# Up projections of two feed-forward blocks as seven block products instead of eight, over two halves of the tokens

## What is computed

```
def half_ffn(x, g, w_up, w_down):          # x: tokens x 1024, w_up: 1024 x 5632, w_down: 2816 x 1024
    a, b = jnp.split(rmsnorm(x, g) @ w_up, 2, axis=-1)
    return x + 0.5 * ((jax.nn.silu(a) * b) @ w_down)
```

## Time and profile before

| | us |
|---|---|
| median of three runs | 2714.2 (2714.13 to 2714.91) |
| the profiled execution, whole | 2714.25 |
| its span in the profile | 2712.2 |
| mean granted TensorE clock of that execution | 0.982 of full speed |
| TensorE busy | 2630.6 |
| VectorE, ScalarE, GpSimd busy | 1008.2, 726.6, 718.8 |

### The profile page before, as it was taken

How to read it: one execution, slowest core, us unless ns; L and a number is a source line. 1 busy time by engine, 2 the same in 40 slices (tenths; PEclk the granted TensorE clock), 3 DMA queues, 4 the chain that set the end, 5 groups by cost and what they waited for, 6 DMA issues and landing times. The chain is left out here.

```text
span 2712.2 us, 37487 instructions
## 1 busy us (share of the span) xinstructions
PE 2630.6 (97%) x15304; PEld 2563.0 (94%) x15304; DVE 1008.2 (37%) x2105; ACT 726.6 (27%) x1276; POOL 718.8 (27%) x400
## 2 busy tenths in 40 slices
PE   7999999999999999999998998998999999999998
PEld 6999999999998899999987778998999999999997
DVE  5022222221117237998635642324022222222116
ACT  5111111111113332212547753223111111111112
POOL 5222222222222211212223103325222222222221
PEclk8999999999998999999998998998999999999999
DMA  4111111111103221213333404512111111111102
GB/s 133 47 47 41 38 47 47 33 46 47 44 19 103 73 67 58 65 49 100 94 85 73 76 1 134 169 32 63 47 47 47 32 47 47 41 37 47 47 16 78
DMA packets 208890, 160.42 MB, mean 59 GB/s; under 512 B 34844, under 2 KB 192600, under 8 KB 208608
## 3 DMA queue, kind: packets, MB, share of 16 engines
q1 hardware_dynamic: 208736, 158.16, 20.1%
HBM read 130.94 MB, written 25.99 MB: 58 GB/s over the span
## 5 line engine op out<-in xcount | busy, mean ns | idle before, releaser
L372 PE MATMUL f1ps_up<-xn_lo,f1w_hi 128*128 128x384 f32 x1056 | 353.9, 335 | 8.5 <-POOL xn_lo L327 8.5
L372 PE MATMUL f2ps_up<-xn_lo,f2w_hi 128*128 128x384 f32 x1056 | 354.3, 335 | 7.1 <-POOL xn_lo L327 7.1
L373 PE MATMUL f2ps_up<-xn_hi,f2w_lo 128*128 128x384 f32 x1056 | 353.7, 335 | 0.0
L374 PE MATMUL f2ps_up<-xn_hi,f2w_hi 128*128 128x384 f32 x1056 | 353.7, 335 | 0.0
L373 PE MATMUL f1ps_up<-xn_hi,f1w_lo 128*128 128x384 f32 x1056 | 353.5, 335 | 0.0
L374 PE MATMUL f1ps_up<-xn_hi,f1w_hi 128*128 128x384 f32 x1056 | 353.5, 335 | 0.0
L372 PE MATMUL d_ps<-xn_lo,d_w_hi 128*128 128x384 f32 x864 | 298.6, 346 | 6.5 <-POOL xn_lo L327 4.9
L373 PE MATMUL d_ps<-xn_hi,d_w_lo 128*128 128x384 f32 x864 | 293.6, 340 | 0.0
L374 PE MATMUL d_ps<-xn_hi,d_w_hi 128*128 128x384 f32 x864 | 293.5, 340 | 0.0
L530 DVE TENSOR_TENSOR f2hid<-f2gate,f2ps_up 128x384 f32<-128x384 f32 x66 | 36.6, 555 | 503.2 <-ACT f2gate L499 503.2
L530 DVE TENSOR_TENSOR f1hid<-f1gate,f1ps_up 128x384 f32<-128x384 f32 x66 | 36.6, 555 | 503.1 <-ACT f1gate L499 503.1
(11 more groups left out here) (357 smaller groups left out, 5178.8 us busy)
## 6 DMA issues: line engine op xcount, KB each, us to landing
f1raw<-in_w_ffn_up SPq DMA_DIRECT2D x44, 512.0 KB
f2raw<-in_w_ffn_up SPq DMA_DIRECT2D x44, 512.0 KB
d_raw<-in_w_in SPq DMA_DIRECT2D x35, 512.0 KB, 5.1
p_dram<-stage SPq DMA_DIRECT2D x24, 576.0 KB, 3.2
f1raw<-in_w_ffn_down SPq DMA_DIRECT2D x11, 1024.0 KB
f2raw<-in_w_ffn_down SPq DMA_DIRECT2D x11, 1024.0 KB
b_sg<-p_dram SPq DMA_DIRECT2D x16, 576.0 KB, 4.9
x_dram<-xT SPq DMA_DIRECT2D x1, 4608.0 KB, 15.1
```

The source lines that it names most:

```text
L372: nc.tensor.matmul(out, w_hi, x_lo, start=first, stop=False)
L373: nc.tensor.matmul(out, w_lo, x_hi, start=False, stop=False)
L374: return nc.tensor.matmul(out, w_hi, x_hi, start=False, stop=final)
```

## The change

Both `ffn` calls are replaced. The token axis is cut into two halves of 576 (`HT`), each of two quarters of 288 (`QT`). The weights are loaded, and split, once for each half. A tile of an up projection is 1024 rows by 256 columns of `w_up`, seen as a 2 by 2 matrix of blocks (512 by 128); the normalised tokens of a half are a 2 by 2 matrix of blocks too (512 rows by 288 tokens). Their product takes seven block products (Strassen's scheme in the form with shared sums) where eight would do it directly. Four of the seven weight operands are differences of blocks (`terms`), four of the seven token operands are sums or differences (`combine`), and the four result blocks are sums of the seven products (`add`). One block product is 4 k-blocks by 3 matmuls of 288 columns, 12 matmuls; a down step is 12 matmuls of 288 columns as well (2 quarters, 2 hidden blocks, 3). The order of steps, for each half:

```diff
+    RING, RAWS, TS = 9, 3, 4
+    ORDER = [tile for g in range(NG) for tile in (("a", g), ("b", g), ("d", g - 1)) if tile[1] >= 0] + [("d", NG - 1)]
...
+    FREED = {LAST[j - RING]: j for j in range(RING, len(LAST))}
...
+    EDGE = STEP[0, "d", NG - 2]
```

On VectorE, which runs for every step s: `evict`, then `ahead(FREED[s])`, then `rest(s)`:

```diff
+                def terms(tile, which):
...
+                        if q:
+                            dve.wait_ge(t_ok, q)
+                        a, b = [(part(n, 0, 1), part(n, 0, 0)), (part(n, 1, 1), ts[:, (q - 1) % TS]),
+                                (part(n, 1, 1), part(n, 0, 1)), (part(n, 1, 0), ts[:, (q - 2) % TS])][i]
+                        v.tensor_tensor(ts[:, q % TS], a, b, ALU.subtract).then_inc(t_ok, 1)
...
+                        terms(tile, {0: (0, 1), 1: (2,), 4: (3,)}.get(x, ()))
...
+                    for dst, src in {1: ((1, 0),), 2: ((0, 0),), 3: ((2, 0),), 4: ((3, 2), (0, 0)), 5: ((0, 0),),
+                                     6: ((2, 2),)}[m]:
+                        v.tensor_tensor(ev[:, b + dst], ev[:, b + src], bank(s), ALU.add).then_inc(ad_ok, 1)
...
+                    v.tensor_tensor(product(x), ev[:, AT[x]], product(x), ALU.mult).then_inc(hm_ok, 1)
...
+                    dve.wait_ge(hh_ok, 4 * group(h, g) + x + 1)
+                    v.tensor_tensor(hidden(h_lo, h, g, x), product(x), hidden(h_hi, h, g, x).bitcast(F32), ALU.subtract)\
+                        .then_inc(hl_ok, 1)
...
+                    if kind == "d":
+                        dve.wait_ge(mm_ok, s + 1)
...
+                        v.scalar_tensor_tensor(x, ps[:, b:b + 2, 0:QT], 0.5, x, ALU.mult, ALU.add).then_inc(dn_ev, 1)
+                        return
+                    if m:
+                        add(G, s, kind, m)
+                    if kind == "b" and m in (1, 4, 5, 6):
+                        multiply(G, {1: 0, 4: 1, 5: 2, 6: 3}[m])
+                    if kind == "b" and m == 4:
+                        hidden_lo(h, g, 0)
+                    if kind == "b" and m == 6:
+                        hidden_lo(h, g, 1)
```

On the other engines:

```diff
+                def split_lo(j):
+                    pool.wait_ge(hi_ok, j + 1)
+                    nc.gpsimd.tensor_tensor(slot(w_lo, j), source(j), slot(w_hi, j).bitcast(F32), ALU.subtract)\
+                        .then_inc(lo_ok, 1)
+                    pool.wait_ge(lo_ok, j + 1)
...
+                def down(s, h, g, m):
...
+                    if 8 * G + m >= 2:
+                        pe.wait_ge(dn_ev, 8 * G + m - 1)
```

More of the change, by code:

```diff
@@ L374, in product3, with ffn @@
     return nc.tensor.matmul(out, w_hi, x_hi, start=False, stop=final)
-def ffn(nc, ctx, M, K, w_up, w_down, gain, xT, xn_hi, xn_lo, tag, summed):
+def ffn(nc, ctx, M, K, w_up, w_down, gain, xT, tag, summed):
     sem = lambda n: ctx.enter_context(nc.semaphore(tag + n))
[L387 to L391, removed]
-    with ExitStack() as mem, M.scope():
[L393 to L413, removed]
@@ L454, in run, with bank @@
[L454 to L471, removed]
+        def bank(s):
+            return ps[:, UPS.index(s) % 4, 0:QT]
@@ new lines, in added, with group, part, hidden @@
+        def added(G, kind, n):
+            return 14 * G + (7 if kind == "b" else 0) + n
+        def group(h, g):
+            return NG * h + g
+        def part(n, row, col):
+            r = raw[:, n % RAWS].rearrange("p (k n) -> p k n", k=KT)
+            return r[:, 4 * row:4 * row + 4, col * P:(col + 1) * P]
+        def hidden(t, h, g, x):
+            f, i = ((0, 0), (1, 1), (1, 0), (0, 1))[x]
+            return t[:, group(h, g) % 2, f, i * QT:(i + 1) * QT]
+        def product(x):
+            return ev[:, 4 + AT[x]]
@@ new lines, in _ @@
+                norm.root(act)
+                norm.rows(act)
+                for k in range(4):
+                    if k < 2:
+                        split_hi(k)
+                    for which in "ABS":
+                        norm.high(act, 0, k, which)
+                for j in range(2, RING):
+                    split_hi(j)
+                for s, step in enumerate(STEPS):
+                    evict(s, *step)
+                    if s in FREED:
+                        split_hi(FREED[s])
+                    rest(s)
@@ new lines, in _ @@
+                for k in range(4):
+                    if k < 2:
+                        split_lo(k)
+                    x_low(0, k, "A")
+                    x_low(0, k, "B")
+                for j in range(2, RING):
+                    split_lo(j)
+                for s, step in enumerate(STEPS):
+                    if s in FREED:
+                        split_lo(FREED[s])
+                    if EDGE <= s < EDGE + 16:
+                        k, r = divmod(s - EDGE, 4)
+                        if r == 1:
+                            x_low(1, k, "A")
+                            x_low(1, k, "B")
+                        if r == 3:
+                            x_low(1, k, "S")
@@ new lines, in _ @@
+                norm.inverse(dve)
+                norm.diagonals(dve)
+                for k in range(4):
+                    norm.apply(dve, 0, k)
+                    norm.combine(dve, 0, k, range(4))
+                    if k == 1:
+                        ahead(0)
+                    if k:
+                        norm.low(v, dve, 0, k - 1, "S")
+                norm.low(v, dve, 0, 3, "S")
+                for j in range(1, RING):
+                    ahead(j)
+                for s, step in enumerate(STEPS):
+                    evict(s, *step)
+                    if s in FREED:
+                        ahead(FREED[s])
+                    rest(s)
@@ L585, in project @@
+                norm.sums(pe)
+                norm.spread(pe)
+                for s, (h, kind, g, m) in enumerate(STEPS):
+                    if kind == "d":
+                        down(s, h, g, m)
+                    else:
+                        up(s, h, kind, g, m)
 def project(nc, ctx, M, K, io, out, xT, x_dram, xn_hi, xn_lo, kvT, DM, mix, aq_at, kvT_at, mix_at, scratch, g_dram, E):
```

477 lines of the change are left out of this document (329 added, 148 removed).

## The result

The kernel after takes 2902.4 us (median of 4 runs, 2901.1 to 2903.7), the kernel before 2714.4: a ratio of 1.069 (95% interval 1.067 to 1.071), slower by 188 us, where 2840 was forecast. The profiled execution spans 2900.6 us.

A forecast was written before the change was run, and what follows sets the result against it. TensorE's feed-forward matmuls were taken to bound the kernel. From 2714.25 us, -119.5 for fewer columns, +172 for stalls before d2, +36 for starts, +36 for middles and +1 for end evictions gave 2840; range 2640 to 2935.

The forecast's parts named there:

- Slower: Whole kernel: the chance given to the change making it slower, 0.71, against same 0.04 and faster 0.25.
- The lock of VectorE and GpSimd: Steady groups: VectorE operations with two SBUF operands and GpSimd's SBUF-reading ones exclude each other, delaying d2 by 4.3 us.
- VectorE keeps up: Rival, b tile: lock waits fit the slack, stall 0.1 us, up to 1.3; 2636 to 2690 us, chance 0.22.
- half the waits: Rival, b tile: stalls of only 2 to 3 us a pair; 2700 to 2780 us, chance 0.12.
- the hand schedule: b tile: both queues laid out one after the other, giving 5.4 us of lock waits for ten VectorE operations.
- the likeliest case: Whole kernel: VectorE late by the lock, 2790 to 2890 us, chance 0.50.
- the clock falls as well: Rival, after stalls before d2: half clock for 5 us costs 2.3 each, 92 in all; 2890 to 2935 us, chance 0.14.
- TensorE's columns: Feed-forward blocks: 5808 matmuls of 288 columns at 0.1315 us replace 4752 at 0.1733, saving 119.5 us (108 to 137).
- the left end of the line: Matmul time: 256 columns at mean 0.1175 us, joined by a line to 384 columns to give 0.1315 at 288.
- The stalls: d2 after a b tile: TensorE waits 4.3 us for VectorE's eviction of d0, 40 times, +172 us (4 to 196).
- The edges: Starts and middles: VectorE's list with lock waits delays TensorE, +18 us a block (10 to 24) and +18 (8 to 22).
- Hidden: Weight loads: loading twice, 69 MB a block at 81 GB/s, stays covered and costs TensorE nothing.

The follow-up runs named there:

- e1: Kernel after with GpSimd's subtraction for the weights' low parts replaced by a memset that reads nothing (output lacks them): 2674.6 us, 0.985 of the kernel before.
- e9: e1 with three more memsets per weight slot, keeping GpSimd about as busy as in the kernel after but reading nothing: 2676.2 us, 0.986 of the kernel before.
- e10: Kernel after with each GpSimd subtraction for a weight slot made as two instructions of half the elements: 2757.9 us, 1.016 of the kernel before.
- e6: e5 with the token sums in idle PSUM banks and their low parts in the middle on VectorE, not GpSimd: 2706.2 us, 0.997 of the kernel before.
- e3: Kernel after with 26 thrown-away matmuls ahead of TensorE's wait before d2: 2853.5 us, 1.051 of the kernel before.
- e5: Kernel after with the next a tile's terms moved to a4, a5, b0 and `hidden_lo` to d1 to d4 (not last groups): 2715.3 us, 1.000 of before.
- e11: e8 with the halved GpSimd instructions of e10: 2700.3 us, 0.995 of the kernel before.
- e4: Kernel after with the four `hidden_lo` subtractions of a group back on GpSimd: 2802.7 us, 1.032 of the kernel before.
- e8: e6 with the low part of the sums made one d step after the scaling in a block's middle: 2691.1 us, 0.991 of the kernel before.

## Why the prediction was right or wrong

**Direction and mechanism: right.** Slower had 0.71. The lock of VectorE and GpSimd, the place (the eviction of d0, wanted by d2), the operations that are stretched (terms, multiplications, `hidden_lo`) and those that are not were as told; e1, e9 and e10 show the cause by taking away the reading, keeping the busy time, and halving the length. The Trainium skill ("SBUF — State Buffer", section "SBUF: two separate sides") has it that the two lock each other out for a whole instruction; the rows of e6 and e10 agree, and 466 to 467 ns beside a median of 1063 is its sharpest case here. The rivals *VectorE keeps up* and *half the waits* fell: the ten waits of the b tile shown were 5.6 us where the hand schedule gave 5.4. The time itself, 2902, lies above the band of the likeliest case (2790 to 2890) and in the one given to *the clock falls as well* (2890 to 2935, 0.14).

**TensorE's columns: over-sized by 21 us.** 0.1315 us was taken, with 0.1325 as the end; it is 0.1333, and 98.6 us were saved in place of 119.5. The rows named for the left end of the line, give 0.115 (0.23 us for two matmuls) and not 0.1175. The value itself is borne out by the other pairs of 256 columns in the trace of before:

```profile
961.62 0.28 PE L1114 MATMUL d_ps_s<-d_k_hi,d_qs 128*128 128x256 f32 x1
961.75 0.28 PE L1115 MATMUL d_ps_s<-d_k_lo,d_qs 128*128 128x256 f32 x1
961.86 0.40 PE L1114 MATMUL d_ps_s<-d_k_hi,d_qs 128*128 128x512 f32 x1
...
967.25 0.28 PE L1114 MATMUL d_ps_s<-d_k_hi,d_qs 128*128 128x256 f32 x1
967.37 0.28 PE L1115 MATMUL d_ps_s<-d_k_lo,d_qs 128*128 128x256 f32 x1
967.49 0.40 PE L1114 MATMUL d_ps_s<-d_k_hi,d_qs 128*128 128x512 f32 x1
```

A pair takes 0.24 us here, and the four pairs of the trace together 0.94 us for eight matmuls, 0.1175 each. So the step that failed is the straight line from two matmuls that stand alone between other shapes to a long stream: a stream of 288 columns takes 1.8 ns more than the line says. From 384 to 288 columns the time falls by 40 ns, which is 96 columns at 2.4 GHz, the granted clock here; of the 133 ns, 13 do not shrink with the columns. Why the pairs of 256 columns lie 2 to 3 ns below the line through these two streams stays open. The Trainium skill ("TensorE: Matmul & The Clock Gate", section "Back-to-back issue gap") gives 122.5 ns for 288 columns, as the gap of a single, isolated matmul; the stream here takes 133, and the measurement decides.

**The stalls: 137 in place of 172 us.** 3.72 us each, 4.4 in the first group of a half, where 4.3 was taken (3.8 to 4.9). On the timeline VectorE takes 14.5 us from the result of b1 (301.11) to the end of the eviction of d0 (315.66; the row at 314.92 holds two evictions). Of it 5.6 are waits, so its own list is 8.9 us where 10.2 was summed: each handing over was priced at 0.05 us, but an operation often starts some 0.08 us before the end of the one ahead (305.85 against 305.93). There are 36, not 40: that of the last group of a first half merges with the middle, and the last group of the second half has no terms to make and does not stall.

**The clock: 64 us that the sum left out.** The slow matmuls of both blocks, 636, cost 0.107 us more than others, 68 us, of which some 4 were there before. This is the main miss. The mechanism was among the rivals, with 0.14 and 92 us, and the earlier trace rows had priced it. It was put up as another outcome in place of an addition to the likeliest one, although the likeliest one had 40 stalls of the very length at which those rows show the fall. With it at its measured size the sum would have been 2904. It came after 15 of the 18 stalls of the first block, at 1.4 to 2.4 us each (13 to 22 times 0.107) where 2.3 was priced; e3 shows it by itself.

**The edges: 22 and 21 us a block where 18 and 18 were taken**, both within their ends (10 to 24, 8 to 22). The first matmul started earlier than before, at 29.03 in place of 32.06; the gaps stand behind it, as here, the third and fourth part of the tokens:

```profile
40.66 0.61 PE L458 MATMUL f1ps<-f1xs_lo,f1w_hi 128*128 128x288 f32 x1 [6.05 <-POOL f1xs_lo L452]
46.83 0.61 PE L458 MATMUL f1ps<-f1xs_lo,f1w_hi 128*128 128x288 f32 x1 [5.08 <-POOL f1xs_lo L452]
```

**Hidden: right.** No wait of TensorE is ended by a DMA of the weights; their second load is hidden at 80 GB/s.

The misses by size: +21 (columns), -35 (stalls), +64 (clock), +8 and +6 (edges) make +64; 2902 is 62 over 2840. That -35 and the +35 of columns and edges cancel is luck: with only the stalls priced rightly the forecast would have been 2805.

## What to carry to other kernels

Work taken off the bounding engine is paid for on the others, and their busy share does not tell whether they can bear it: here TensorE lost 137 us to VectorE at 67% and, in the steady groups, nothing to VectorE at 70% (e5), by where in the schedule the operations with two SBUF operands stood. Look for the stretch in which the result that TensorE needs next is made, sum VectorE's list there with half an instruction of GpSimd for each two-operand operation, and move out what is not needed in it, put an operand into PSUM, or cut GpSimd's instructions where GpSimd itself has room (e10 gained by it, e11 lost). Where the sum has stalls of some microseconds, add the fall of the clock behind them in the same case.

## What the runs showed of the hardware that was not expected

In the first block the clock fell after 15 of 18 idle times of 3.6 to 4.3 us before d2, and in e4 after 2 of 16 of 2.1 us; in the kernel after each fall cost 13 to 22 matmuls at 0.240 us. So the stalls of 4 us cost nearly half as much again, and those of e4 little more than their own length. The length alone does not decide: stalls of the same 3.7 us come with and without slow matmuls, and in the middle of a block of e8 and e10 a run of 13 or 14 of them also stands behind gaps of 2.1 to 2.3 us. What separates them is open. Matmuls that are thrown away hold the clock (e3). And a memset of GpSimd leaves VectorE's terms at their free 684 ns, at nearly the same busy time at which a subtraction doubles them (e9).
